# Matmuls of two token groups issued together, each weight piece named twice in a row

## The reference

```python
z = rmsnorm(x, g) @ w_in          # (2048 + 128) tokens, 1024 -> 7424 columns
qa, ka, va, ga, qb, kb, vb, gb, qc, gc, gm = jnp.split(z, split_points(IN_SIZES), axis=-1)
kv = rmsnorm(mem, g_mem) @ w_mem_kv   # 256 memory tokens, 1024 -> 1024 columns
```

## Time and profile before

| | |
|---|---|
| median of 3 runs | 3466.63 us (3464.53 to 3466.77) |
| profiled execution, span | 3459.2 us |
| PE busy | 3060.3 us (88%), 19677 matmuls and 19677 weight loads |
| DVE, ACT, POOL busy | 1390.7, 977.8 and 701.2 us |
| projection, matmuls at L305 | from 78.7 to 1462.6 us |

### The profile page before, as it was taken

One profiled execution on the slowest core, in us unless ns is written; L12 is line 12 of the kernel. 1 busy time (PEld: TensorE's weight loads), 2 busy tenths in 40 slices (PEclk: granted clock), 3 DMA queues, 4 the chain that ended last, 5 costly groups with the idle time before them and its releaser, 6 DMA issues. The chain is left out here.

```text
span 3459.2 us, 51587 instructions
## 1 busy us (share of the span) xinstructions
PE 3060.3 (88%) x19677; PEld 2517.3 (73%) x19677; DVE 1390.7 (40%) x1953; ACT 977.8 (28%) x1793; POOL 701.2 (20%) x576
## 2 busy tenths in 40 slices
PE   5999999999999999842898997998977966999798
PEld 4888888888888888822676675766756743978687
DVE  6000000000000000230898897998975631543333
ACT  5111111111111111112444444454436842210121
POOL 0000000000000000031343443443433530333100
PEclk7999999999999999975998999999998986999899
DMA  4122122122222212377645656454555640754443
GB/s 153 57 76 76 57 76 76 61 71 76 68 64 76 76 57 76 93 260 224 207 168 164 188 168 186 166 172 146 165 165 145 173 123 23 220 196 159 163 139 115
DMA packets 301571, 442.95 MB, mean 128 GB/s; under 512 B 23200, under 2 KB 184736, under 8 KB 291184
## 3 DMA queue, kind: packets, MB, share of 16 engines
q1 hardware_dynamic: 279632, 327.48, 30.5%
q0 software_dynamic: 21792, 113.52, 10.0%
HBM read 326.64 MB, written 114.29 MB: 127 GB/s over the span
## 5 line engine op out<-in xcount | busy, mean ns | idle before, releaser
L305 PE MATMUL prj_bank<-hidden_hi,prj_w_hi 128*128 128x512 f32 (+2 forms) x2384 | 848.1, 356 | 11.7 <-DVE prj_w_lo L289 10.8
L305 PE MATMUL prj_bank<-hidden_lo,prj_w_hi 128*128 128x512 f32 (+2 forms) x2384 | 847.7, 356 | 0.0
L305 PE MATMUL prj_bank<-hidden_hi,prj_w_lo 128*128 128x512 f32 (+2 forms) x2384 | 847.0, 355 | 0.0
L287 DVE CAST prj_w_hi<-prj_w 128x1024 fp32r<-128x1024 f32 x66 | 46.0, 696 | 1259.6 <-PE prj_bank L305 1247.2
L305 PEld LDWEIGHTS prj_bank<-hidden_hi,prj_w_hi 128*128 128x128 f32 x2384 | 448.2, 188 | 68.2 <-issue 11.5
L340 ACT ACTIVATE prj_z<-prj_bank 128x512 f32<-128x512 f32 x290 | 155.0, 534 | 1194.5 <-PE prj_bank L305 1194.5
L305 PEld LDWEIGHTS prj_bank<-hidden_hi,prj_w_lo 128*128 128x128 f32 x2384 | 448.2, 188 | 54.9
L305 PEld LDWEIGHTS prj_bank<-hidden_lo,prj_w_hi 128*128 128x128 f32 x2384 | 448.3, 188 | 54.5
L942 POOL TENSOR_TENSOR stk_beta<-stk_beta,stk_left 128x1024 f32<-128x1024 f32 (+4 forms) x160 | 282.3, 1765 | 471.6 <-DVE stk_left L857 471.6
L355 POOL DMA_DIRECT2D scratch_zT<-prj_z x58 | 31.0, 535 | 1407.0 <-ACT prj_z L340 1407.0
L806 ACT ACTIVATE stk_beta<-stk_z 128x1024 f32<-128x1024 f32 (+2 forms) x224 | 181.9, 812 | 350.1 <-PE stk_z L993 271.4
(11 more groups left out here) (215 smaller groups left out, 4258.0 us busy)
## 6 DMA issues: line engine op xcount, KB each, us to landing
stk_kd<-in_cache_sb_k SPq DMA_DIRECT2D x64, 1024.0 KB, 7.2
stk_vd<-in_cache_sb_v SPq DMA_DIRECT2D x64, 1024.0 KB, 5.3
scratch_zT<-prj_z POOLq DMA_DIRECT2D x58, 1088.0 KB, 5.4
prj_w<-in_w_in SPq DMA_DIRECT2D x58, 512.0 KB, 5.9
mrg_gate<-scratch_zT SPq DMA_DIRECT2D x24, 768.0 KB, 4.4
rot_z<-scratch_zT SPq DMA_DIRECT2D x14, 1088.0 KB, 6.1
mrg_u_raw<-scratch_uT SPq DMA_DIRECT2D x9, 1024.0 KB, 8.9
fin_a_raw<-scratch_mgT SPq DMA_DIRECT2D x17, 512.0 KB, 4.9
```

The lines of the kernel that those rows point to most:

```text
L305: last = pe.matmul(out, w[u][:, k, :], h[:, k, first:first + width], start=(k == 0 and w is w_hi and h is hi), stop=(k == KC - 1 and w is ...
```

## The change

`products` takes a list of groups, and inside a k and a product it issues one matmul for each of them. PE's loop calls it for the groups (0, 1), then (2, 3), then 4 alone. The waits of both groups of a pair stand ahead of the pair; their conditions are as before. Each group's own last matmul raises `summed`. The memory tokens use the new function with one group.

```diff
-            def products(out, u, first, width):
+            def products(u, groups):
                 for k in range(KC):
                     for w, h in ((w_hi, hi), (w_hi, lo), (w_lo, hi)):
-                        last = pe.matmul(out, w[u][:, k, :], h[:, k, first:first + width],
-                                         start=(k == 0 and w is w_hi and h is hi),
-                                         stop=(k == KC - 1 and w is w_lo))
+                        for out, first, width, sums in groups:
+                            last = pe.matmul(out, w[u][:, k, :], h[:, k, first:first + width],
+                                             start=(k == 0 and w is w_hi and h is hi),
+                                             stop=(k == KC - 1 and w is w_lo))
+                            if sums is not None and k == KC - 1 and w is w_lo:
+                                last.then_inc(sums, 1)
                 return last
...
-                    for g, (first, width) in enumerate(GROUPS):
-
-                        if g == 0:
-                            pe.wait_ge(emptied[u], 5 * j)
-                        elif u == 0 and g == 1:
-                            pe.wait_ge(emptied[1], 5 * j)
-                        elif u == 1 and g >= 3:
-                            pe.wait_ge(emptied[0], 5 * j + g - 1)
-                        last = products(bank[banks_of[u][g]][:, 0:width], u, first, width)
-                        last.then_inc(summed[u], 1)
+                    for together in ((0, 1), (2, 3), (4,)):
+                        for g in together:
+                            if g == 0:
+                                pe.wait_ge(emptied[u], 5 * j)
+                            elif u == 0 and g == 1:
+                                pe.wait_ge(emptied[1], 5 * j)
+                            elif u == 1 and g >= 3:
+                                pe.wait_ge(emptied[0], 5 * j + g - 1)
+                        products(u, [(bank[banks_of[u][g]][:, 0:GROUPS[g][1]], *GROUPS[g], summed[u]) for g in together])
...
-                    products(bank[banks_of[u][0]][:, 0:MEM], u, TOK, MEM).then_inc(summed[u], 1)
+                    products(u, [(bank[banks_of[u][0]][:, 0:MEM], TOK, MEM, summed[u])])
```

## The result

The changed kernel takes 3500.65 us (median of 4, 3499.01 to 3502.46), the one before beside it 3466.31 us: slower by 34 us, ratio 1.01, 95% interval 1.0085 to 1.0114. The forecast was 3489 us in a range of 3478 to 3502. The direction and the larger of the two costs held; the loss is half as large again as the sum of +22 us, and a quarter of it was not in the sum.

What follows compares the result with a forecast made beforehand. PE was taken to bound the projection, busy 1290.00 of 1290.00 us. Repeated weights, bank changes, other waits and clock at 0 plus 28 holes of 0.80 us gave 3466.6 + 22.4 = 3489 us, range 3478 to 3502.

Steps and rivals of the forecast that it cites:

- the sum of +22 us: Projection loop turns: 28 holes of 0.80 us each, 22.4 us in all, between 19.3 and 31.6.
- What bounds the stage: Projection: PE has no idle time, so only the distance between matmul starts or a hole between them can change its length.
- The other waits cost nothing: Projection, waits other than at the loop turn: evictions awaited in u = 1 are over some 17 us earlier; cost 0.
- Repeated weights, other bank, cost 0: Paired matmuls in the projection: naming the same weights again, in another bank, neither drops a load nor shortens a step; 0.
- rivals A: Pairs: a second naming of weights in another bank is free of its load, 49 us back, 3440 us; 9 in 100.
- Rival B: Pairs: two matmuls into one bank pay 13 ns, into two don't; 73 us faster, 3416 us; 3 in 100.
- The lost cover: Loop turn: group 0's 24 matmuls no longer stand ahead of the wait for the last block's eviction; 0.80 us, 28 times.
- the direct case of the earlier trace: Loop turn, ACT's end to PE's first weight load: 0.06 us, taken from where the blocking wait is last before the matmul.
- Rival C: Loop turn: holes as long as today's before the memory products, 1.13 us, 28 times, 3498 us; 20 in 100.
- Cost 0 as well: Projection steps into another bank: 0.15 us behind a 320-column matmul, as inside the group, so changing banks costs 0.
- the 7.4 us between span and median of before: Whole kernel: median of the runs 7.4 us above the profiled span of 3459.2 us, used to turn span into run time.
- The forecast's own range: Whole kernel: 3484 to 3494 us around 3489, for holes of 0.7 to 0.95 us; 62 in 100.

## Why the prediction came out as it did

**What bounds the stage.** Right. A change of the matmul's distance or a hole between them was all that counted; the phases behind only started later. The other waits cost nothing, as forecast (the eviction awaited in u = 1 is over some 22 us ahead by the steps, not 17, which changes nothing): PE's idle time for ACT in the stage is the 28 turns and the one of before.

**Repeated weights, other bank, cost 0.** Right, against rivals A and B. The trace of before held each half of it; the kernel without any repetition and the equal pairs on other banks closed the combination that it didn't hold. The second of them is the strongest: with the costs removed, the gain that was meant to be under them is 0 within 3 us. Rival B counted 95 new bank changes a block; they are 92, since two of the 94 inside the pairs were there before, which lifts its time by 2 us and changes nothing else.

**The lost cover.** Right in place, in count (28) and in what ends it. The term was 0.80 us. In the changed kernel the turn costs 0.86 to 0.87 us read at the matmuls. In the round of the kernel with one pair it is 0.83 us, because there the wide matmuls behind the hole are spared the slow steps (0.02 us) that they have directly behind a 320-column group; in the changed kernel steps behind the hole are slow as well. The part that was short is the one from ACT's end to the load: 0.06 us as the direct case of the earlier trace rows, measured 0.11. The assumption was that the blocking wait, the last in the program, is carried by the load; it became an instruction of its own, and the satisfied one was carried. With the waits exchanged the hole is as the sum had it. Rival C, 1.13 us, had the right kind of doubt and a size seven times too large: without a loop entry the extra between ACT's end and the load is 0.05 us, not 0.34.

**What was missing: the mixed pair.** The step that failed is "Cost 0 as well" for the alternation of groups. It was argued from a bank change between groups and excluded a longer step "to 0.01 us". That bound was too coarse for something paid 1392 times: 0.0061 us x 48 a round are 0.29 us, 8.5 us over the stage. The earlier trace rows moreover showed the step into a wide matmul and one step behind it (0.23), in which 6 ns can't be seen at two digits. Five steps read together there would have shown 0.02 us, a sign that a narrow matmul ahead costs a wide one something, though not the price of taking turns, which the trace of before doesn't hold.

**The sum.** 23 us of hole + 8.5 us of mixed pair = 32 us; the round gives 33, the runs 34 (the interval goes from 29 to 40). In the profiled execution the span is 38.8 us longer. Of the excess 2 us lie in the memory products, where PE waited once for weights that landed late, and 3 us behind the projection, where nothing was changed. The prediction took the 7.4 us between span and median of before for a fixed distance. In the changed kernel the same execution has a time of 3499.68 us and a span of 3498.0, 1.7 us apart; so the profiled execution of before was probably some 5 us faster than the median, which isn't shown, as its own time is not on record.

**The range** held the time, but that was luck in part. The forecast's own range, 3484 to 3494 us, was missed by 7 us. The time fell into the upper part, which was meant for rival C, and the mixed pair, which the sum put at nothing, took it there.

**What stays open:** why two widths in turn cost 6 to 7 ns a pair of matmuls and two equal widths of 512 or 320 nothing, and why 416 next to 416 costs 3 ns (0.15 / 48). Repetition, order in the pair, first column and which banks are used are excluded by runs, and alternating banks alone costs nothing at equal widths of 512 or 320. No run alternates widths within one bank, so whether the width does it alone or only together with the change of bank isn't shown; what in the engine it is, no row here shows.

## What to carry to other kernels

Before matmuls are regrouped for the sake of their weights, look whether a repetition that is already there is any shorter or has fewer loads; here the answer stood in three rows. When two accumulation groups are opened together, the first matmul inherits the waits of both, so the bank that is freed last should go to a later group. And an order that is repeated a thousand times needs its step read over many instances, to the nanosecond: 6 ns were a quarter of the loss.

## What the runs showed of the hardware

- A wait costs differently by where it ends up: with the blocking wait on the load 0.04 to 0.05 us from ACT's end to the load, with it as an instruction ahead 0.11 us. The order of the waits in the program decided it here: of the two waits for ACT, the load carried the first and not the last.
- Matmuls of alternating widths take 6 to 7 ns more a pair than the same ones in runs of equal width (0.380 against 0.3733 us for 512 and 320 columns). Behind a run of 320 columns the next five steps of 512-column matmuls are slow by some 0.02 us together (five steps of 0.230 against 0.227 us).
- Holes in which PE waits 0.6 us for an eviction, 0.93 us from start to start, once in 48 us leave the granted clock at 1.00, the 2.4 GHz level, from 90 to 1380 us.
- The part of the program behind the projection, unchanged in all kernels, took between 1992 and 2005 us in the profiled executions (span less the start of the last matmul at the projection's line). A single profile can't tell 10 us in this kernel; the round could tell 0.04 us.
